# Second block's attention: scores behind older values in mid-chunk, probabilities scaled behind the turned copies

## What is computed

```python
def latent_window_attention(q, k, v, ck, cv, sink):
    s_loc = jnp.einsum('bnqhgd,bnkhd->bnhgqk', qb, kw) * scale      # 128 queries, 3 blocks of 128 keys
    s_loc = jnp.where(valid[None, :, None, None], s_loc, NEG_INF)
    s_ctx = jnp.einsum('bnqhgd,bchd->bnhgqc', qb, ck) * scale       # 256 context keys
    p = jax.nn.softmax(jnp.concatenate([s_loc, s_ctx, s_sink], axis=-1), axis=-1)
    ...

def second_block(...):
    for l in range(DEPTH):
        ...
        px = hx @ w_in[l]
        q, k, v, u, gv, f = jnp.split(px, [Q_END, K_END, V_END, U_END, G_END], axis=-1)
        attn = latent_window_attention(q, k, v, ck, cv, sink[l])
        sgu = spatial_gating(jax.nn.gelu(u), jax.nn.gelu(gv), w_sgu[l], b_sgu[l], g_sgu[l])
        four = fourier_mix(f)
        y = merge_heads(attn, sgu, four, g_mix[l], w_out[l])
        x = x + g1 * rmsnorm(y, g_post_mix[l])
        ...
```

## Time and profile before

| | us |
|---|---|
| median of 3 runs (lowest, highest) | 3984.42 (3980.23, 3987.14) |
| span of the profiled execution | 3985.4 |
| PE busy in it | 3701.6 (93%) |
| VectorE, ACT, POOL busy | 2124.2, 1725.2, 1777.2 |
| steps 6 to 11 of layer 0, in the projection | 60.31 |
| steps 14 to 23 of layer 0, ten DFT points | 74.14 |
| step 24 to the start of step 31, layer 0 | 67.99 |

### The profile page before, as it was taken

The page is one execution under the profiler, slowest core; times in us unless marked ns, Lnnn a source line. Parts: engine busy times, 40 slices in busy tenths (PEclk is TensorE's granted clock), DMA queues, the critical chain, the costliest instruction groups (busy, mean ns, idle before and its releaser), DMA issues.

```text
span 3985.4 us, 61376 instructions
## 1 busy us (share of the span) xinstructions
PE 3701.6 (93%) x22388; PEld 2990.2 (75%) x22388; DVE 2124.2 (53%) x3355; ACT 1725.2 (43%) x2899; POOL 1777.2 (45%) x1288
## 2 busy tenths in 40 slices
PE   4999999999997899888999999999899899999997
PEld 3867767777775777667888997887777778887886
DVE  5546546556456576667224654336567673245234
ACT  2355355354354454554224453335455552243233
POOL 1544435344343422335445885554322354455444
PEclk8999999999998999989999999999999999999998
DMA  6433434333423321112322453322221223222322
GB/s 252 132 122 127 145 118 137 126 137 132 140 103 106 110 69 54 59 54 90 100 95 91 154 173 100 95 95 81 94 69 54 68 81 95 93 92 95 95 95 100
DMA packets 127221, 421.32 MB, mean 106 GB/s; under 512 B 17280, under 2 KB 19104, under 8 KB 126368
## 3 DMA queue, kind: packets, MB, share of 16 engines
q1 hardware_dynamic: 121488, 410.09, 31.4%
q10 hardware_dynamic: 5520, 8.34, 0.6%
HBM read 397.40 MB, written 6.29 MB: 101 GB/s over the span
## 4 chain that ended last, share of the span: by engine, by line
PE 54%; DVE 7%; ACT 3%; issue 2%; POOL 0%; DMA 0%; SPq 0%; ACTq 0%; DVEq 0%; POOLq 0%
PE lin L2674 30%; PE lin L2683 15%; PE bankO L2799 2%; PE lin L2932 2%; PE bankT L2741 2%; DVE x L2319 1%; DVE tmp L2285 1%; DVE y L2318 1%; PE scores L2774 1%; DVE h_lo L2308 1%; DVE staged L2297 1%; ACT whi L1904 1%; PE lin L2816 1%; PE lin L2704 0%; PE scores L2775 0%
## 5 line engine op out<-in xcount | busy, mean ns | idle before, releaser
L1885 POOL TENSOR_TENSOR wlo<-late_raw,whi 128x512 fp32r<-128x512 f32 x456 | 642.5, 1432 | 766.6 <-PE lin L2683 498.6
L1885 POOL TENSOR_TENSOR wlo<-wraw,whi 128x512 fp32r<-128x512 f32 x452 | 636.3, 1431 | 713.3 <-PE lin L2683 497.8
L2674 PE MATMUL lin<-h_hi,whi 128*128 128x512 f32 (+1 forms) x1896 | 714.9, 384 | 48.9 <-ACT f L2198 12.6
L2674 PE MATMUL lin<-h_lo,whi 128*128 128x512 f32 (+1 forms) x1896 | 701.5, 377 | 0.0
L523 POOL TENSOR_TENSOR wlo<-wraw,whi 128x512 fp32r<-128x512 f32 x260 | 356.4, 1392 | 465.7 <-PE lin L1168 280.2
L2674 PE MATMUL lin<-a_hi,whi 128*128 128x512 f32 (+1 forms) x1280 | 472.1, 376 | 11.9 <-ACT tmp L2207 7.9
L2674 PE MATMUL lin<-a_lo,whi 128*128 128x512 f32 (+1 forms) x1280 | 469.3, 374 | 0.0
L2674 PEld LDWEIGHTS lin<-h_hi,whi 128*128 128x128 f32 x1896 | 368.5, 194 | 133.6 <-issue 24.7
L1904 ACT ACTIVATE whi<-late_raw 128x1024 fp32r<-128x1024 f32 x228 | 239.1, 1057 | 516.5 <-PE lin L2674 411.3
L1904 ACT ACTIVATE whi<-wraw 128x1024 fp32r<-128x1024 f32 x226 | 237.3, 1057 | 499.0 <-PE lin L2674 416.0
L2683 PE MATMUL lin<-h_hi,wlo 128*128 128x512 f32 (+1 forms) x1896 | 439.3, 375 | 1.2 <-POOL wlo L1885 0.7
(11 more groups left out here) (381 smaller groups left out, 6428.1 us busy)
## 6 DMA issues: line engine op xcount, KB each, us to landing
wraw<-in_w SPq DMA_DIRECT2D x332, 512.0 KB, 3.5
late_raw<-in_w SPq DMA_DIRECT2D x212, 512.0 KB, 3.5
mod_ring<-in_w_ada SPq DMA_DIRECT2D x96, 512.0 KB, 4.6
mod_ring<-in_w_mod SPq DMA_DIRECT2D x32, 512.0 KB, 4.7
tmp<-tmp SPq DMA_DIRECT2D x224, 64.0 KB, 2.0
first_ring<-in_w_mod SPq DMA_DIRECT2D x16, 512.0 KB, 16.5
wraw<-in_dft_tokens SPq DMA_DIRECT2D x16, 512.0 KB, 3.6
late_raw<-in_dft_tokens SPq DMA_DIRECT2D x16, 512.0 KB, 3.6
```

What stands on the lines that cost most here:

```text
L1885: last = nc.gpsimd.tensor_tensor(wlo[:, s, half], raw_chunk[r][:, half], whi[:, s, half].bitcast(F32), ALU.subtract)
L2674: last = nc.tensor.matmul(bank[s][:, 0:p.w], whi[:, s, k * P:(k + 1) * P], h[:, k, 0:p.w], start=(k == 0 and h is parts[0]), stop=False)
```

## The change

Nothing is added or left out; the order in four queues is another.

- PE: `begin` is gone. `middle` now issues the values of step i-2 and then the score of step i, in the middle of the chunk or the point.
- ACT: `exponentials(l, i)` stands behind `turned(l, i - 1, 0)`. In the projection that is behind `refill` (the split of weight chunk i+2), in the DFT points ahead of the squares, the high parts and the two `split_high`, in all stages ahead of what follows the end of the chunk's products.
- VectorE: `attended(l, i - 2)` stands ahead of `maximum(l, i)`. In the projection both stand behind the rotation, gate, squares and scalings of the chunk instead of at its head. `normalize(l, i)` stands behind `turned(l, i - 1, 1)`, at the end of the step.

```diff
 # ACT, project
-                    if attending:
-                        exponentials(l, s)
                     if s < last:
                         refill(p.in_at + s, s)
                     if attending:
                         turned(l, s - 1, 0)
+                        exponentials(l, s)
 # ACT, fourier: dimension halves, then DFT points
+                    turned(l, i - 1, 0)
                     exponentials(l, i)
-                    turned(l, i - 1, 0)
...
-                    exponentials(l, i)
                     if h == 11:
                         mix_roots(first)
                     turned(l, i - 1, 0)
+                    exponentials(l, i)
 # ACT, merge
-                    exponentials(l, i)
                     if prev and k == 0:
                         root_post(prev)
...
                     turned(l, i - 1, 0)
+                    exponentials(l, i)
 # VectorE, project
-                        if attending:
-                            maximum(l, s)
-                            attended(l, s - 2)
...
                         if attending:
+                            attended(l, s - 2)
+                            maximum(l, s)
                             turned(l, s - 1, 0)
+                            turned(l, s - 1, 1)
                             normalize(l, s)
-                            turned(l, s - 1, 1)
 # VectorE, fourier (both parts) and merge, in each
+                    attended(l, i - 2)
                     maximum(l, i)
-                    attended(l, i - 2)
...
                     turned(l, i - 1, 0)
-                    normalize(l, i)
...
                     turned(l, i - 1, 1)
+                    normalize(l, i)
 # PE
-            def begin(l, i):
-
+            def middle(l, i):
+
+                if 0 <= i - 2 < STEPS2[l]:
+                    values(l, i - 2)
                 if i < STEPS2[l]:
                     score(l, i)
-
-            def middle(l, i):
-
-                if 0 <= i - 2 < STEPS2[l]:
-                    values(l, i - 2)
 # PE, project, both parts of fourier, merge
-                    begin(l, i)
```

More of the change, by code:

```diff
@@ L2715, in _ @@
             h_parts, a_parts = (h_hi, h_lo), (a_hi, a_lo)
-            def begin(l, i):
-                if i < STEPS2[l]:
-                    score(l, i)
             def middle(l, i):
@@ L2725, in middle @@
                     values(l, i - 2)
+                if i < STEPS2[l]:
+                    score(l, i)
             def turn(l, i, kv, also=None):
@@ L2849, in project @@
                     if attending:
-                        begin(l, s)
                         between = partial(middle, l, s)
```

## The result

| | before | after |
|---|---|---|
| median of the runs, us | 3982.32 (4 runs) | 4131.55 (4 runs) |
| lowest, highest | 3973.21, 3987.14 | 4124.24, 4139.43 |
| span of the profiled execution | 3985.4 | 4122.5 |
| ratio, 95% interval | | 1.0373 [1.0353, 1.0394] |

What follows compares the result with a forecast made beforehand. TensorE was taken to bound the kernel, busy 3701.6 of 3985.4 us. Layer 0's +34 and layer 1's +41 gave +75; with 14 for the clock, +89, hence 4073 us, range 4025 to 4112.

Steps and rivals of the forecast that it cites:

- 14 for the clock: DFT pairs: TensorE's clock halves after idle stretches; half of 16 pairs hit at 1.7 us each, bounds 0 to +37.
- the +32 of the DFT stage: DFT points, per layer: weight splits and turned copies queue behind later exponentials and maximum; +32 us, from 20 to 42.
- that of the merges: Merge products: late normalizing shortens the values waits and switches gain; -7 us in layer 0, -1.5 in layer 1.
- Sign (1): Even DFT points: PE waits 2 to 3 us for ScalarE's split weights, some 8 per layer; pairs about 17.3 us.
- the loop: Projection chunks: rotation, maximum, exponentials, raw copy and DMAs close a cycle of 11.4 us against 9.45 of PE work.
- Rival (b): Projection: the rotation loop doesn't bind, so -4 us per layer instead of +7.8, 4049 us; chance 0.14.
- The last three pairs and the entry to the merges: End of the DFT stage: roots wait +3.7, three scalings +3.5, work queued at the end +6.8 us.
- Points 7 to 10: DFT points with two squares each: +3.5 us for squares behind exponentials, +2 for VectorE's additions holding copy and sums.
- sign (3): Merges: the waits for values shrink to under half.
- rival (c): The clock falls at nearly every stall: +37 us instead of +14, 4096 us, up to 4110; chance 0.15.
- Sign (5): DFT stage: more stretches with TensorE's clock at 0.50.
- GpSimd beside VectorE: DFT points: GpSimd's splits slow VectorE's normalizing by 0 to +16 us in all; taken at 0, 6 by the skill's rule.

Runs made afterwards that it cites:

- `max_before_rotation`: The changed kernel, with VectorE taking the output copy and the maximum ahead of the rotation in projection steps 5 and 7 to 10: 4109.48 us, ratio 1.0312.
- `scales_behind_copy`: The changed kernel with squares ahead of the exponentials, plus VectorE's gate and mixed-row scaling at points 12 to 14 between the two turned copies: 4083.07 us, 1.0243.
- `sums_before_low`: The changed kernel with squares ahead of the exponentials, plus the last DFT sums copied ahead of VectorE's low parts and scaling at point 15: 4083.16 us, 1.0240.
- `merge_normalize_last`: The kernel before, with the scaling of the probabilities behind the second turned copy in the merge chunks alone: 3983.15 us, ratio 0.9991.

## Why the prediction was right or wrong

- **Which step failed.** Added up by stages, the loss is 73 us in layer 0 and 65 in layer 1, where the prediction had 34 and 41 and another 14 for the clock: 49 us too little. The DFT stage makes 23 of them (51.6 and 49.8 measured, for 32 in each layer and the clock's 14), the merges 18.5, the dimension halves 4, the projection 3. So the term of the sum that was mis-sized is the +32 of the DFT stage, and the term that was wrong in kind is that of the merges.
- **Direction and mechanism of the DFT pairs: right.** Pair 17.13 at full clock (17.35 predicted), split wait 2.38 (2.7), points 0 to 9 +20.9 and +20.6 per layer (+18 without the clock). Sign (1) of the prediction's list is there: 8.6 us of waits for `whi` in four.
- **The projection: right in sum.** Chunks 6 to 11 +11.2 and +11.9 (+11.5 predicted). Chunks 0 to 5 gave 2.3 us in layer 0 and some 2 in layer 1 (-3.7 predicted): the first score gave more than the 2.5, and chunks 2 to 5 lost 1.8 where chunks 0 to 5 were to win 1.2. A chunk without special work did fall from 9.65 to 9.46, which is the 0.2 taken for the switch; chunks 2 and 4 took 0.8 and 1.4 longer. `max_before_rotation` shows the loop to be the main part of the loss: 7 of the 11 to 12 us in each layer go with it. Rival (b) falls.
- **The last three pairs and the entry to the merges: mis-sized.** Predicted +14 per layer (3.7 + 3.5 + 6.8), measured 9.8 + 10.2 + 4.9 + 5.9 = +30.7 in layer 0 and +29.2 in layer 1. The working has one price for each of these pairs, for what is special in it, the roots, the scalings, the end; the 2.5 that every pair pays isn't among them. The runs bear this out for points 12 and 13: of 10.2, `scales_behind_copy` takes back 4.2 (3.5 predicted for the scalings), the squares ahead take 1.4, and 4.5 are left. Points 10 and 11: of 9.8, the squares ahead take 6.4, and 3.4 are left; no run shows the roots apart, for which 3.7 was taken. For the entry the working had seen that the scaling stands in front of the copy, and took 6.8 for points 14 and 15 with it; the copy also stands behind a wait for ScalarE's high parts, and the two stretches lost 10.8. `sums_before_low` takes 14.3 back over both layers.
- **Points 7 to 10: named, but followed too short a way.** +5.5 for squares and additions; taking the squares ahead gave 14.2 in points 7 to 11 of layer 0 and 11.5 in layer 1. What was missed is that VectorE's waiting addition holds the scaling, behind which the sums are copied, until GpSimd's splits begin.
- **Merges: wrong sign.** -7 predicted for layer 0, measured +7.2 in chunks 2 to 9 and +1.3 in chunk 10; -1.5 predicted for layer 1, +1.5 measured in its chunk 2. The prediction took the gain of the late scaling (`merge_normalize_last` has 90.00 for 91.20 there) but not the late score and exponentials in the same chunks: alone, VectorE's part takes 89.44 there, but PE's 99.95 and ScalarE's 95.33. The waits for values in the merges rose from 10.4 to 15.1, where sign (3) had them under half. The squares ahead take back only 1.9 of the 7.2 (96.53 for 98.42); the rest wasn't taken apart.
- **The dimension halves:** +3.9 in each layer, +1.5 and +2.5 predicted: the low parts stand behind the maximum in both halves, where the prediction let the context's products cover one. PE's part alone already gives 20.18 (ScalarE's alone 16.49).
- **The clock:** +14 predicted, PE's busy time grew 34.7, near the upper bound of 37. This looks like rival (c), which alone would have given 4096 to 4110, but how much of the 34.7 lies on the path isn't measured. At point 2 it does, with 1.5 us where 1.7 was taken. The idle time grew by 102.4, against the 75 predicted for it. Sign (5) is there: mean granted clock 0.78 to 0.90 in points 7 to 15, where before has 1.00 in each of these stretches.
- **GpSimd beside VectorE:** taken at 0. At point 7 it costs 0.93 + 1.76 = 2.7 and at point 15 some 0.6 + 0.8 = 1.4 (and 0.9 on a low part, 1.62 for 0.68) ahead of a copy of sums that PE waits for, nearly the same in both layers, so some 8 to 10 us. The estimate of 6 in the prediction by the rule of the Trainium skill (SBUF — State Buffer, Who interferes with whom), that the two engines shut each other out for a whole instruction, was nearer than my 0. The trace agrees with it in that the wait lands on the sum and the scaling of an odd point behind which sums are copied, but only at points 7 and 15; at points 3 and 11 of layer 0 these take 0.15 and 1.02 as ever.
- **Small sums.** The 5.0 after which PE is done with an odd point are 5.1 by their terms, which changes nothing.
- **The range** was too narrow above because its upper end held only the clock's bound over a sum whose DFT term had been given an upper bound (42 per layer, found 50 to 52) that never entered the range together with it.

## What to carry to other kernels

Moving an operation to a later place in an in-order queue is paid by whatever now stands behind it, on its own engine and one engine on: list these neighbours for each kind of step (first, regular, with norm squares, last) and cost each kind in full, the regular price plus the special one. A reordering can be worth keeping in some steps only: the same three moves gained some 2 us in the first six steps of a layer and lost 4 to 12 us in each later stage. A stage is compared between two traces from the same instruction, not from the same time. And where each part of a change is costed alone, check that the parts don't need each other: here they cost 184, 43 and 124 us apart and 149 together.

## What the runs showed of the hardware that was not expected

- The same list of instructions in chunks 6 to 11 took 71.5 us in some of the kernels and 78.0 in others that differ only later, with PE busy 62.5 or 66.4 and a mean granted clock of 0.95 or 0.89. A stage's duration in one profiled execution can carry some 6 us of this.
- VectorE's busy time rose by 25.2 us for the same number of instructions. A part of it is seen beside GpSimd's splits, where two scalings that take 1.02 took 2.78 and a sum of 128x2 took 1.08 for 0.15.
- The same even point of the DFT, behind the same wait of 2.38 us, took 11.49 us at a mean granted clock of 0.85 and 9.95 at 1.00. Unused products in the wait brought 11.49 down to 9.95 where they stood ahead of what PE waited for, and added up to 7.3 us where they stood behind it.
